# Value products of two attention heads issued together, turn by turn, in every second step

## The reference, cut to what matters

```python
def one_block(qblk):
    s = jnp.einsum('bqhd,bkhd->bhqk', qblk, k).astype(jnp.float32) * scale
    p = jax.nn.softmax(s, axis=-1)
    return jnp.einsum('bhqk,bkhd->bqhd', p.astype(v.dtype), v)
```

## Time and profile before

| what | value |
|---|---|
| median of three runs | 1052.37 us (1051.87 to 1052.90) |
| span of the profiled execution, first to last instruction | 1048.6 us |
| profiled execution's own time | not on the page; the median lies 3.8 us above the span |
| PE busy | 98% of the span, 93% of the chain that ended last |
| DVE, ACT, POOL busy | 60%, 42%, 10% |
| attention of layer 0, of layer 1 | 190.5 to 232.4 us, 697.1 to 738.1 us |

### The profile page before, as it was taken

One profiled execution on the slowest core, in us unless ns is written; L12 is line 12 of the kernel. 1 busy time (PEld: TensorE's weight loads), 2 busy tenths in 40 slices (PEclk: granted clock), 3 DMA queues, 4 the chain that ended last, 5 costly groups with the idle time before them and its releaser, 6 DMA issues.

```text
span 1048.6 us, 16439 instructions
## 1 busy us (share of the span) xinstructions
PE 1026.5 (98%) x6552; PEld 938.2 (89%) x6552; DVE 632.1 (60%) x1134; ACT 439.6 (42%) x684; POOL 106.0 (10%) x99
## 2 busy tenths in 40 slices
PE   7899999999999999999999999999999999999995
PEld 4698995789999989999999999668999999999995
DVE  6686868868555543534448787886765555543333
ACT  3256445446333332343334655644543333233231
POOL 0004323003000000000100223400200000000100
PEclk9999999999999999999999999999999999999998
DMA  9843245214333478333364224451243333633331
GB/s 383 330 168 124 82 161 216 115 44 165 129 131 133 168 285 321 118 112 114 135 243 161 91 88 161 161 203 41 81 142 134 125 120 120 258 105 111 126 122 60
DMA packets 30678, 159.56 MB, mean 152 GB/s; under 512 B 3424, under 2 KB 4384, under 8 KB 19872
## 3 DMA queue, kind: packets, MB, share of 16 engines
q1 hardware_dynamic: 28896, 146.75, 38.4%
q10 hardware_dynamic: 1728, 12.06, 2.8%
HBM read 156.27 MB, written 2.52 MB: 151 GB/s over the span
## 4 chain that ended last, share of the span: by engine, by line
PE 93%; DVE 3%; ACT 1%; issue 1%; ACTq 1%; DVEq 0%
PE ps L475 26%; PE ps L477 26%; PE ps L476 26%; PE ps L504 3%; PE ps L920 2%; PE ps L900 1%; PE ps L719 1%; PE ps L746 1%; PE ps L909 1%; PE ps L571 1%; PE ps L823 1%; ACTq L1065 1%; PE ps L802 1%; PE ps L710 0%; DVE wlo L1353 0%
## 5 line engine op out<-in xcount | busy, mean ns | idle before, releaser
L475 PE MATMUL ps<-h_hi,whi 128*128 128x386 f32 (+1 forms) x1120 | 384.9, 344 | 0.2
L477 PE MATMUL ps<-h_hi,wlo 128*128 128x386 f32 (+1 forms) x1120 | 379.7, 339 | 0.0
L476 PE MATMUL ps<-h_lo,whi 128*128 128x386 f32 (+1 forms) x1120 | 378.7, 338 | 0.0
L1353 DVE TENSOR_TENSOR wlo<-stage,whi 128x2048 fp32r<-128x2048 f32 (+1 forms) x106 | 223.3, 2106 | 154.4 <-ACT whi L1015 154.4
L1015 ACT ACTIVATE whi<-stage 128x2048 fp32r<-128x2048 f32 (+1 forms) x106 | 185.9, 1754 | 229.1 <-PE ps L477 210.5
L475 PEld LDWEIGHTS ps<-h_hi,whi 128*128 128x128 f32 x1120 | 211.3, 189 | 9.7 <-issue 7.2
L476 PEld LDWEIGHTS ps<-h_lo,whi 128*128 128x128 f32 x1120 | 211.6, 189 | 0.3
L477 PEld LDWEIGHTS ps<-h_hi,wlo 128*128 128x128 f32 x1120 | 210.6, 188 | 0.0
L475 PE MATMUL ps<-hid_hi,whi 128*128 128x384 f32 x352 | 118.3, 336 | 0.0
L477 PE MATMUL ps<-hid_hi,wlo 128*128 128x384 f32 x352 | 118.3, 336 | 0.0
L476 PE MATMUL ps<-hid_lo,whi 128*128 128x384 f32 x352 | 118.3, 336 | 0.0
(11 more groups left out here) (295 smaller groups left out, 1146.4 us busy)
## 6 DMA issues: line engine op xcount, KB each, us to landing
stage<-wf_dram SPq DMA_DIRECT2D x44, 1024.0 KB, 4.8
adas<-wada_dram SPq DMA_DIRECT2D x80, 512.0 KB, 5.7
stage<-wf_dram SPq DMA_DIRECT2D x32, 704.0 KB, 4.1
stage<-win_dram SPq DMA_DIRECT2D x20, 1024.0 KB, 4.8
stage<-wout_dram SPq DMA_DIRECT2D x8, 1024.0 KB, 5.8
adaf<-wada_dram ACTq DMA_DIRECT2D x6, 1024.0 KB, 15.0
small<-small_dram SPq DMA_DIRECT2D x2, 1202.5 KB, 8.5
stage<-win_dram ACTq DMA_DIRECT2D x2, 1024.0 KB, 13.2
```

The lines of the kernel that those rows point to most:

```text
L475: mm(out, ah, bh, start=(k == 0), stop=False)
L476: mm(out, ah, bl, start=False, stop=False)
L477: return mm(out, al, bh, start=False, stop=(k == n - 1))
L1353: tt(wlo[:, g % 2, 0:width], stage[:, g % 2, 0:width], whi[:, g % 2, 0:width].bitcast(F32), ALU.subtract)\
```

## The change

The value products are no longer issued in every step from the third, one pair (block, head) at a time. In the even steps 4, 6, 8, 10, 12 and 14 the products of two pairs, a = i-4 and a = i-3, are issued as one group. These two always belong to one block of queries and to two neighbouring heads, of which the first writes to the partitions 0 to 63 and the second to 64 to 127. Within the group the products take turns: key tile by key tile, first head, second head. The odd steps have no value products. `my_ps` is counted once for each group. The transposed probabilities get four buffers, in the blocks 1 and 2 of `adas`, and ACT waits for a group that lies two groups back instead of for a pair that lies two pairs back.

```diff
-            pr, pt = (adas[:, b, 0:2 * T].rearrange("p (b t) -> p b t", b=2) for b in range(2))
+            pr = adas[:, 0, 0:2 * T].rearrange("p (b t) -> p b t", b=2)
+            pt = adas[:, 1:3, 0:2 * T].rearrange("p a (b t) -> p a b t", b=2)
...
-                    if 0 <= i - 3:
-                        a = i - 3
-                        c, h = ATT[a]
+                    if i >= 4 and i % 2 == 0:
+                        pair = (i - 4, i - 3)
+                        c, h0 = ATT[pair[0]]
                         k0, nk = keys(c)
-                        pe.wait_ge(pt_ready, L * NATT + a + 1)
-                        o = (h % 2) * 64
-                        if a == 0:
+                        pe.wait_ge(pt_ready, L * NATT + pair[1] + 1)
+                        if i == 4:
                             pe.wait_ge(halved, L * 2 + 2)
                         for kt in range(nk):
-                            last = mm(ps[o:o + 64, 5 + h // 2, c * P:c * P + P], vm[:, k0 // P + kt, h * 64:h * 64 + 64],
-                                      pt[:, a % 2, kt * P:kt * P + P], start=(kt == 0), stop=(kt == nk - 1))
+                            for a in pair:
+                                h, o = ATT[a][1], a % 2 * 64
+                                last = mm(ps[o:o + 64, 5 + h0 // 2, c * P:c * P + P],
+                                          vm[:, k0 // P + kt, h * 64:h * 64 + 64],
+                                          pt[:, a % 4 // 2, a % 2, kt * P:kt * P + P], start=(kt == 0), stop=(kt == nk - 1))
                         last.then_inc(my_ps, 1)
...
-                        if a >= 2:
-                            act.wait_ge(my_ps, L * NATT + a - 1)
-                        f(pt[:, a % 2, 0:nk * P], ps[:, 2 + a % 2, 0:nk * P], ACT.Copy).then_inc(pt_ready, 1)
+                        if a >= 4:
+                            act.wait_ge(my_ps, L * (NATT // 2) + a // 2 - 1)
+                        f(pt[:, a % 4 // 2, a % 2, 0:nk * P], ps[:, 2 + a % 2, 0:nk * P], ACT.Copy).then_inc(pt_ready, 1)
...
-                act.wait_ge(my_ps, L * NATT + NATT)
+                act.wait_ge(my_ps, (L + 1) * (NATT // 2))
```

## The result

The changed kernel takes 1046.9 us (median of four runs, 1046.3 to 1049.23) beside 1052.39 us (1051.87 to 1052.9); the ratio is 0.9942 with a 95% interval of 0.9925 to 0.9959. The profiled execution took 1046.3 us, with a span of 1043.4 us where it was 1048.6. Predicted were 1047.0 and 1043.2 us. Measured again later (experiment 10), the ratio is 0.9965 (0.9953 to 0.9978).

A forecast was written before the change was run, and what follows sets the result against it. PE, 98% busy, bounds the kernel, with chains through DVE and ACT close behind. Without waits 5.0 us a layer; with them 2.71, 2 x 2.71 = 5.4, so 1052.4 to 1047.0 us; range 1045 to 1049, chance 0.78.

The forecast's parts named there:

- V(6, 7): Value products of pairs 6 and 7, steps 9 and 10: start 0.87 us early, set by the copy of pair 7.
- T(9): Transpose of pair 9's probabilities in step 11: waits for DVE's scaling, so starts only 0.68 us early.
- The price of a group: Two heads' value products, priced from the state-space scan: 0.37 us for 4 records, 0.81 for 12; second head 0.01.
- "lost" 2.3 us a layer: Attention: 5.0 us a layer without waits, 2.71 with them; 0.45 lost in steps 3 and 4, 0.7 in 7 and 8.
- the waits named: PE's waits for DVE's scaling at the transposes of pairs 6, 8 and 9 in the attention, claimed longer; no size each.
- longer waits for ACT's copy: Sign of being right: PE waits longer for ACT's copy at the value products of pairs 4, 5 and 6, 7; no size.
- the shift of the chain from step 8 on: DVE and ACT chain from pair 8's maximum, which follows the addition before it: moves 0.68 us earlier.
- the second rival: Behind the attention, the gain is given back at a weight split: 1049.7 us for one layer, 1052.4 for both; chance 0.07.
- a longer wait behind the attention: Sign of being wrong: PE waits longer after the last value products than before; no size given.
- PE alone (1): Attention: the other engines' chains give way and the full 10.0 us comes, 1042.4 us; chance 0.05.
- No overlap (3): Value product groups: heads run one after the other at 0.11 us a record; 1.4 us gained, 1051.0 us; chance 0.05.
- draining (4): Value product groups: each change of half drains PE, 0.20 us a record instead of 0.11; slower, 1059 us; chance 0.05.

The follow-up runs named there:

- experiment 10: The changed kernel measured once more with no edit, against the kernel before: 1048.23 us, ratio 0.9965.
- experiment 5: The changed kernel with DVE's weight split moved from the end of step 8 to the end of step 9: 1046.79 us, 0.9945 against the kernel before.
- experiment 7: The changed kernel with the older pair first in each step on DVE (scaling before maximum) and ACT (copy before exponential): 1047.67 us, 0.9959 against the kernel before.
- experiment 8: The changed kernel with the edits of experiment 5 and experiment 7 together: 1044.88 us, 0.993 against the kernel before.
- experiment 11: The kernel of experiment 8 with the PSUM banks of the output projection's first two second-half tiles exchanged: 1042.7 us, 0.9916 against the kernel before.
- the ninth experiment: The changed kernel with GpSimd adding only one column of 384 in the mixer output's sum of squares, so the second norm is not computed: 1045.9 us in one run.
- the first experiment: The changed kernel with all key tiles of a group's first head before those of the second, no turns: 1047.87 us, 0.9955 against the kernel before.

## Why the prediction was right, and where not

It was right in its result (1046.9 for 1047.0 us) and in its mechanism. That the two medians come so close is luck: four executions of the changed kernel lie 2.9 us apart, and in the repeat the gain is 1051.59 - 1048.23 = 3.4 us, where 5.4 were forecast. The times within a layer, which repeat within 0.05 us, tell more. By the prediction's steps, with the 0.13 us by which S(0) starts later in the changed kernel's layer 0 added to the difference of the starts:

| place | start before | start after | early | predicted |
|---|---|---|---|---|
| V(0, 1) | 198.98 | 199.00 | 0.11 us | 0.11 us |
| S(7) | 208.64 | 208.12 | 0.65 | 0.64 |
| V(4, 5) | 211.68 | 210.85 | 0.96 | 0.94 |
| V(6, 7) | 219.88 | 219.03 | 0.98 | 0.87 |
| T(9) | 221.43 | 220.76 | 0.80 | 0.68 |
| last group | 229.85 | 227.14 | 2.84 | 2.71 |

- **The price of a group** was read from another part of the kernel, and came out to the hundredth: 0.37 and 0.81 us. That decided the sum.
- **Most of the "lost" 2.3 us a layer was lost to the waits named:** T(6), T(8) and T(9) wait for DVE, as said, and T(2) does too. Experiments 5, 7, 8 and 11 then showed what they hang on, by taking it away, for all but T(2). Where the prediction spoke of longer waits for ACT's copy it was not: PE waits for T first, and by the time it is at V the copy is at most 0.25 us behind, so that wait stayed at 0.5 us in total.
- **The mis-sized term** is the shift of the chain from step 8 on, 0.68 us, which measured 0.11 and 0.12 more at V(6, 7) and T(9). It assumed that DVE's maximum starts when the addition before it ends. DVE's timeline after:

```profile
210.16 0.74 DVE L1415 SCALAR_TENSOR_TENSOR x<-ps,modl,x 128x128 f32<-128x128 f32 x2
210.81 0.55 DVE L1773 TENSOR_REDUCE att<-ps 128x1 f32<-128x384 f32 x1
```

  The maximum starts at 210.81, while the addition ends at 210.90: the overlap of 0.09 us that was named as unknown, at its upper end.
- **Not foreseen: the 0.44 us given back in layer 0,** the second rival in small, by a cause that it didn't name; a longer wait behind the attention was among its signs of being wrong. By luck the two misses nearly cancel in the span: 2 x 2.71 = 5.4 predicted; 2.84 + 2.89 - 0.43 = 5.3 measured, less 0.13 for the later start, 5.2. The span predicted was 1043.2, and the median was reckoned 3.8 us above it; it lies 3.5 above.
- **The rivals.** PE alone (1) was ruled out by the waits; but experiment 11 shows that its 5.0 us a layer were nearly all to be had by two orders on DVE and ACT, one split and one bank. No overlap (3) and draining (4) are refuted by the 0.81 us. The price of the third, 0.7 us a layer without any overlap, stays untested: even without turns the products overlap in part (1.07 us instead of 1.46), and the kernel then gains 2.28 us a layer.

## What to carry to other kernels

Price a new arrangement of an instruction from a place in the same trace where it already stands, and read it between starts: of a short group the change of shape into and out of it can cost more than the products (some 0.33 of 0.55 us), so two groups made into one save a change of shape as well as what their products overlap. Then walk the path and ask at each step which chain is next; work taken from an engine that is 98% busy came out at 57% here, because chains through the other engines lay close behind. Where a wait moves when its cause is taken away, look for the next cause and change both together: two edits worth 0.2 and -0.3 us alone gave 1.1 together, and with a third 1.9.

## What the runs showed of the hardware that was not expected

- **DVE and GpSimd hold each other up, and which is held can change from layer to layer.** Two operations of L1399 take 0.74 us alone and 1.55 when the second begins within 0.02 us of a GpSimd addition (1.0 us) and is the one held; where GpSimd is held, they keep 0.74 and the addition takes 1.37. DVE's additions from PSUM (L1415) keep 0.73 us beside a GpSimd addition. "SBUF — State Buffer" of the Trainium skill, section "Who interferes with whom", says that a DVE operation with two inputs in SBUF shares a read port with a GpSimd operation that reads SBUF, and that the one issued later blocks until the first is through. L1399 is such an operation and L1415, with one input in PSUM, is not; the rows agree. In the ninth experiment a GpSimd addition of one column begins at 242.17, within DVE's weight split (L1356, two inputs in SBUF, 241.02 to 243.31), and takes 1.19 us instead of 0.19. Where the two start within 0.02 us, the rows do not tell which was issued first: GpSimd's start is the earlier one in all 24 layers.
- **Column halves overlap without turns.** In the first experiment twelve records took 1.07 us, between the 0.81 in turns and the 1.46 of one after the other, since the second head's records start 0.275 us behind the first's and then keep pace. Why 0.275 us isn't settled by these runs.
- **The start of the kernel moves the total more than most edits here.** Windows of 0 to 30 us (length; busy us and instructions of PE, PEld, DVE, ACT and POOL; PE's granted clock; DMA share; GB/s), of the changed kernel and of the first and the fifth experiment:

```profile
0.00:30.00 30.00, 23.27 (x134) 13.14 (x134) 18.35 (x39) 9.62 (x15) 0.21 (x4) 1.00 0.95 390
```

```profile
0.00:30.00 30.00, 24.21 (x126) 13.15 (x127) 17.18 (x37) 8.59 (x13) 0.20 (x4) 0.94 0.95 389
```

```profile
0.00:30.00 30.00, 24.42 (x100) 12.44 (x101) 16.18 (x32) 8.59 (x13) 0.20 (x4) 0.83 0.95 388
```

  The granted clock falls to 0.94 and 0.83 on the mean; for a part of the stretch it is at the lower level, 1.2 GHz instead of 2.4. PE has then got through 126 and 100 records where it otherwise has 134, and S(0) starts at 192.99 and 196.22 us instead of 191.59. The lower level lasts from 18.8 to 22.2 us in the one and from 17.7 to 27.9 in the other. Ahead of it PE had waited 1.6 and 1.7 us for DVE, a wait that the changed kernel's execution has too (1.7 us), without a fall. What tips an execution to either side was not tried. The repeat's 1.55 us (experiment 10) are not of this kind.
